# Gate and up products of three SwiGLU layers read their tokens in pieces of 64 or 32 bytes, in another order in each layer

## The chip, the cores and the metric

The kernel runs on one core of one Trainium2 chip. The metric is the time of one execution on the device, in microseconds (us), as the median of several runs. All the data are float32. TensorE multiplies in the fp32r form: a value is split into a high part and a low part, and a product is made of three matmuls, low by high, high by high and high by low.

## The reference, cut to what matters

The program is two blocks over 512 tokens of width 1024. The first block is a convolution mixer and a SwiGLU; the second has two layers, each with an attention and a SwiGLU whose input product passes a causal convolution of width 3 over the tokens:

```python
h = h + swiglu(rmsnorm(h, g_ffn[l]), w_gate[l], w_up[l], w_down[l])   # first block; 1024 -> 2 x 2816 -> 1024
...
u = x @ w_in                                                          # second block, each layer; 1024 -> 5632
up = jnp.pad(u, ((0, 0), (CONV_WIDTH_2 - 1, 0), (0, 0)))
u = sum(conv_w[j] * up[:, j:j + s] for j in range(CONV_WIDTH_2)) + conv_b
g, val = u[..., :D_FF_2], u[..., D_FF_2:]
return (jax.nn.silu(g) * val) @ w_out
```

The products `x @ w_gate`, `x @ w_up` and the two `x @ w_in` are the ones that the change touches. There are three such stages, named gu0, gu1 and gu2 in the kernel.

## The kernel before, in words

Activations lie with channels on the 128 partitions and the 512 tokens along them: `XH` and `XL` hold the high and the low part of the normed tokens as 8 tiles of 128 channels by 512 tokens. Weights come as items. For a gate or up stage an item is 1024 by 128 weights, that is 8 tiles of 128 by 128, and gives one tile of 128 hidden channels by 512 tokens. A stage has 44 items, 22 gates and 22 ups in turn.

Each item passes through a line of engines. SP's queue loads it into `raw` (two buffers), ScalarE copies it to `WH` in fp32r (line 1585), GpSimd writes the rest, `raw` minus `WH`, into `WL` (line 722), and TensorE runs 8 steps of three matmuls each (lines 963 to 965), accumulating in one PSUM bank of 512 columns. `WH` and `WL` have four slots. The semaphore `w_lo` tells TensorE that a half of an item has its low part, `item_done` gives the slot and the bank on, and `bank_read` tells it that the bank was emptied.

What sets the order is the program of each engine, written out by hand. TensorE's is: `stage_in_halves` does the first two items of a stage in halves of 256 tokens, tile by tile as the norm hands them over (lines 1036, 1048 and 1049), and waits there for all 8 tiles of both halves; `whole` then does the other 42 items of the stage over all 512 tokens, of which the first two go to the banks `attended` and the others to `bank`. A whole item is 24 matmuls of 512 columns, so that the three stages have 3 x 42 x 24 = 3024 of them.

The full banks are read by ScalarE (line 1810 in gu0, line 1939 in gu1 and gu2) and by VectorE (line 2408 in gu0, line 2494 in gu1 and gu2); each reader waits for `item_done` or what follows from it, and reads tokens 0 to 511 in order. The hidden tiles are then split into `HH` (ScalarE) and `HL` (GpSimd, line 849), and the down stage reads these.

`whole` is also called for the other products over all tokens (the mixer's input, the output products); `step` is also called by the attention's projections and by the down stages, through `item`.

Of the kernel before, what the change touches and what calls it, by code (L numbers as in the profile page):

```python
# [9 lines left out]
DT = D // P  # L10
# [39 lines left out]
STAGES = {}  # L50
# [14 lines left out]
FIRST_FOX_STEPS = (0, 0, 1, 1, 2, 2, 2, 2, 2, 2, 2, 0)  # L65
DIFF_STEPS = (1, 1, 1, 1, 2, 2, 2, 3, 2, 4, 5, 0)
FIRST_DIFF_STEPS = (1, 2, 1, 1, 1, 1, 1, 1, 1, 2, 4, 0)
PAIRS = (TAPS + 1) // 2
DIAG_CHUNK = 16
EDGE = (TAPS - 1) // 2  # L70
# [107 lines left out]
def two_blocks(nc, A, out):  # L178
    ctx = ExitStack()
    with ctx:  # L180
        def sb(name, shape, dt=F32, stack=None):
            return (stack or ctx).enter_context(nc.sbuf_tensor(name, shape, dt))
# [20 lines left out]
        WH = sb("WH", [P, SLOTS, DT, P], F32R)  # L203
        WL = sb("WL", [P, SLOTS, DT, P], F32R)
# [17 lines left out]
        first = ExitStack()  # L222
# [9 lines left out]
        mixp = sb("mixp", [P, 2, S], stack=first)  # L232
        tap_f = sb("tap_f", [P, 2, 2 * PAIRS], stack=first)
        tap_h = sb("tap_h", [P, 2, 2 * PAIRS], F32R, stack=first)
        tap_l = sb("tap_l", [P, 2, 2 * PAIRS], stack=first)
        two_ones = sb("two_ones", [P, HEAD], stack=first)
        dg_h = sb("dg_h", [P, 2, 2 * PAIRS, HEAD], F32R, stack=first)
        dg_l = sb("dg_l", [P, 2, 2 * PAIRS, HEAD], F32R, stack=first)
        u_f = sb("u_f", [P, 2, EDGE + HALF], stack=first)
# [66 lines left out]
        banks = bank + ob + sc  # L306
# [402 lines left out]
        def _(pool):  # L709
# [81 lines left out]
            for n in range(12):  # L791
# [3 lines left out]
                if 2 <= n < 6:  # L795
                    g, a = divmod((n - 2) * DIAG_CHUNK, 2 * PAIRS)
                    pool.tensor_tensor(dg_l[:, g, a:a + DIAG_CHUNK, :], two_ones[:, :].unsqueeze(1).broadcast_to([P, DIAG_CHUNK, HEAD]),
# [163 lines left out]
        def _(pe):  # L961
            def product(out_, wh, wl, xh, xl, start, stop):
                pe.matmul(out_, wh, xl, start=start, stop=False)  # L963
                pe.matmul(out_, wh, xh, start=False, stop=False)  # L964
                return pe.matmul(out_, wl, xh, start=False, stop=stop)  # L965

            def step(g, b, hi, lo, k0, k, kt, start, stop, turned=False):

                if k == 0:
                    pe.wait_ge(w_lo, g.times(2).n(2 if turned else 1))  # L970
                if k == kt - kt // 2 and not turned:
                    pe.wait_ge(w_lo, g.times(2).n(2))
                s = g.slot(SLOTS)
                mm = product(banks[b][:, :], WH[:, s, k, :], WL[:, s, k, :], hi[:, k0 + k, :], lo[:, k0 + k, :],
                             start and k == 0, stop and k == kt - 1)
                if k == kt - 1:
                    mm.then_inc(item_done, 1)

            def item(g, b, hi, lo, k0, kt, start, stop):

                for k in range(kt):
                    step(g, b, hi, lo, k0, k, kt, start, stop)

            def bank_free(u):
                pe.wait_ge(bank_read[u.slot(2)], u.round(2))

            def whole(name, j, it=0, per=4, x=(XH, XL), apart=False, fed=False):
                u = Nth(STAGES[name][1] + j, it, per)
                if fed:
                    bank_free(u + -2)  # L990
                elif not apart:
                    bank_free(u)
                item(Nth(STAGES[name][0] + j, it, per), u.slot(2) + 2 * apart, *x, 0, DT, True, True)

            def stage(name, hi=XH, lo=XL):

# [80 lines left out]
            def down(name, layer):  # L1077
# [5 lines left out]
                def tile(t, it=0):  # L1083
                    u = Nth(STAGES[name][1] + t, it, 2)
                    bank_free(u)
                    for j in range(4):
                        if t == 0 and j == 3:
                            for q in h_lo:
                                pe.wait_ge(q, (layer + 1) * FT // 2 + OPEN)
                        item(Nth(STAGES[name][0] + 4 * t + j, it, 8), u.slot(2), HH, HL, *down_part(j), j == 0, j == 3)  # L1090
# [112 lines left out]
            for q in range(QT):  # L1203
                pe.wait_ge(x_in[q], 16)
                for b in range(2):
                    if q == QT - 1:
                        pe.wait_ge(bank_read[b], 1)
                    for t in range(4):
                        mm = pe.transpose(x_banks[q][b][:, t * P:(t + 1) * P], xin[:, q, (4 * b + t) * P:(4 * b + t + 1) * P], ident[:, :])
# [134 lines left out]
            def unit_steps(name, u):  # L1344

                turn0 = STAGES[name][1]
                item0 = STAGES[name][0]
                for tile in range(3):
                    for k in range(DT):
                        part, kk = (tile, k) if tile < 2 else (2 + k // 4, k % 4)  # L1350
                        if k == 0 and tile == 0 and u.base == 1 and isinstance(u.it, int):
                            pe.wait_ge(bank_read[0], turn0 // 2 + 1)
                        elif k == 0 and tile == 1 and u.base == 1 and isinstance(u.it, int) and name == "qkv2":
                            pe.wait_ge(bank_read[1], turn0 // 2 + 1)
                        elif k == 0:
                            bank_free(u.times(4, turn0 + tile))
                        step(u.times(4, item0 + part), tile % 2, XH, XL, k - kk, kk, UNIT[part],
                             part < 3, part != 2, tile < 2 and name == "qkv2")
                        yield

            def unit_steps_fed(name, m):

                stage_in_halves(name, m)
                if name == "qkv1":
                    head_gates()
                turn0, item0 = STAGES[name][1], STAGES[name][0]
                for k in range(DT):
                    step(Nth(item0 + 2 + k // 4), 3 if name == "qkv1" else 2, XH, XL, k - k % 4, k % 4, 4, k < 4, k >= 4)

            def turn_v(name, u):  # L1370

                pe.wait_ge(bank_read[0], u.times(4, STAGES[name][1] + 2).round(2, 1))
                turned = bank[1]
                if name == "qkv2" and first_unit(u):
                    turned = ob[1]
                else:
                    bank_free(u.times(4, STAGES[name][1] + 3))
                for q in range(QT):
                    mm = pe.transpose(turned[:, q * P:(q + 1) * P], vt[:, q * P:(q + 1) * P], ident[:, :])
                mm.then_inc(v_turned, 1)  # L1380
# [43 lines left out]
            def weave(steps, slot_work, counts, lead=0, then=lambda: None):  # L1424

                for _ in range(lead):
                    next(steps, None)
                then()
                for sl, count in enumerate(counts):
                    slot_work(sl)  # L1430
                    for _ in range(count):
                        next(steps, None)
                for _ in steps:
                    pass
# [75 lines left out]
            def diff_slot(u):  # L1510
                slot = u.slot(2)
                first = 4 * UNITS

                def work_of(sl):
                    if sl == 3 and first_unit(u):
                        pe.wait_ge(lam_d, 1)
                    if sl == 1 and not first_unit(u):
                        turn_v("qkv2", u)
                    if sl == 2 and not (isinstance(u.it, int) and u.base == 0):
                        mean_square(u + -1)  # L1520
                    if sl < 8:
                        if sl == 0:
                            pe.wait_ge(q_padded, u.times(128).n(128))
                        if sl < 2:
                            pe.wait_ge(k_low[sl], u.n(1))
                        score(sl, u.times(4, first + sl // 2), slot, sl // 2)
                    if sl in (4, 6, 8, 10):
                        i = sl // 2 - 2
                        turn_map(i % 2, u.times(2, first + i // 2), pmap[:, 2 * (i % 2), :], i)
                    if sl == 11:  # L1530
                        for b in range(2):
                            pe.wait_ge(pt_l[b], u.times(2, first + 2).n() + OPEN)
                        pe.wait_ge(bank_read[1], u.times(4, STAGES["qkv2"][1] + 3).round(2, 1))
                        attend(0, slot, u + UNITS)
                    if sl == 12:
                        mean_square(u)
                return work_of
# [6 lines left out]
            def diff_part(iu, au):  # L1544
# [10 lines left out]
                elif first_unit(au):  # L1555
                    def lambda_and_v():
                        pe.wait_ge(lam_a, 1)
                        pe.matmul(tb[0][:, 0:1], ones[0:1, :], lam_row[2], start=True, stop=True).then_inc(lam_b, 1)
                        turn_v("qkv2", au)
                    weave(unit_steps("qkv2", iu), diff_slot(au), FIRST_DIFF_STEPS, DT, lambda_and_v)  # L1560
                else:
# [1102 lines left out]
```

## Time and profile before

| | us |
|---|---|
| median of 3 runs | 1810.76 |
| lowest and highest of them | 1810.24, 1812.06 |
| profiled execution, its own time | 1809.7 |
| its span | 1807.9 |
| TensorE busy | 1762.5 (97%) |
| weight loads busy (beside the matmuls) | 1476.5 (82%) |
| GpSimd, ScalarE, VectorE busy | 1032.6, 796.2, 765.0 |

The granted clock of TensorE was 0.995 of full speed over the whole execution. A busy time of matmuls is that of records which overlap: a record lasts from the issue until the last column has left the array, and the next matmul starts well before. The pace of a run of matmuls is therefore read from the distance of their starts, not from their length.

### The profile page before, as it was taken

What the parts mean: (1) busy time and instruction counts of PE and PEld (TensorE: products, weight loads), DVE (VectorE), ACT (ScalarE), POOL (GpSimd) and SP (SyncE); (2) the same over time, 40 slices, a digit from 0 to 9 for tenths busy, and PEclk for the clock granted to TensorE, in tenths of its full rate; (3) what the DMA queues carried; (4) which work ended last, traced back from release to release, by engine and by line L of the source; (5) the groups of instructions that cost most, each with busy time, mean ns of one, the idle gap of its engine ahead of it and who ended that gap; (6) DMA issues with size and microseconds to landing.
All of it is one profiled execution on the core that took longest, in us unless ns stands there. A gap on an engine that the chain in (4) does not pass through costs nothing.

```text
span 1807.9 us, 26859 instructions
## 1 busy us (share of the span) xinstructions
PE 1762.5 (97%) x8755; PEld 1476.5 (82%) x8755; DVE 765.0 (42%) x1382; ACT 796.2 (44%) x1674; POOL 1032.6 (57%) x926
## 2 busy tenths in 40 slices
PE   8999999999999999999999999999999999999997
PEld 6879888888887888788888888877777888888887
DVE  7963000002235556553333322487875533333224
ACT  5644323322245555464444422555565644444231
POOL 7966555555562333466666655655554666666651
PEclk9999999999999999999999999999999999999999
DMA  4312333323334454323333233233322233332332
GB/s 154 92 47 83 104 93 93 97 87 108 91 99 106 126 134 117 87 82 98 100 93 93 87 105 94 76 94 82 86 76 76 66 110 98 93 100 83 105 91 98
DMA packets 327252, 171.94 MB, mean 95 GB/s; under 512 B 43458, under 2 KB 316948, under 8 KB 327188
## 3 DMA queue, kind: packets, MB, share of 16 engines
q1 hardware_dynamic: 327172, 171.12, 33.7%
q8 instruction: 35, 0.57, 0.1%
q14 instruction: 29, 0.24, 0.0%
q10 hardware_dynamic: 16, 0.00, 0.0%
HBM read 152.15 MB, written 2.10 MB: 85 GB/s over the span
## 4 chain that ended last, share of the span: by engine, by line
PE 85%; DVE 9%; ACT 2%; issue 1%; POOL 1%; DMA 1%; SPq 0%; DVEq 0%; ACTq 0%
PE bank L963 23%; PE bank L965 23%; PE bank L964 23%; DVE score L2246 3%; PE attended L963 2%; PE attended L965 2%; PE attended L964 2%; PE turned L1404 1%; PE attended L1420 1%; PE bank L1036 1%; PE bank L1048 1%; DVE small L2434 1%; ACT pmap L1841 1%; PE bank L1049 0%; DMA raw<-in_a_w_in 0%
## 5 line engine op out<-in xcount | busy, mean ns | idle before, releaser
L722 POOL TENSOR_TENSOR WL<-raw,WH 128x512 fp32r<-128x512 f32 (+3 forms) x656 | 778.0, 1208 | 542.0 <-ACT WH L1585 539.7
L963 PE MATMUL bank<-XL,WH 128*128 128x512 f32 x1432 | 568.9, 397 | 3.7 <-DVE work L2557 1.2
L965 PE MATMUL bank<-XH,WL 128*128 128x512 f32 x1432 | 557.8, 390 | 0.0
L964 PE MATMUL bank<-XH,WH 128*128 128x512 f32 x1432 | 557.1, 389 | 0.0
L1585 ACT ACTIVATE WH<-raw 128x512 fp32r<-128x512 f32 (+3 forms) x656 | 338.4, 566 | 298.0 <-PE bank L965 177.9
L965 PEld LDWEIGHTS bank<-XH,WL 128*128 128x128 f32 x1432 | 269.4, 188 | 57.0
L963 PEld LDWEIGHTS bank<-XL,WH 128*128 128x128 f32 x1432 | 269.9, 188 | 55.9 <-DVE work L2557 1.5
L964 PEld LDWEIGHTS bank<-XH,WH 128*128 128x128 f32 x1432 | 270.1, 189 | 50.2
L963 PE MATMUL bank<-HL,WH 128*128 128x512 f32 (+1 forms) x528 | 198.6, 376 | 0.0
L965 PE MATMUL bank<-HH,WL 128*128 128x512 f32 (+1 forms) x528 | 198.4, 376 | 0.0
L964 PE MATMUL bank<-HH,WH 128*128 128x512 f32 (+1 forms) x528 | 198.4, 376 | 0.0
L849 POOL TENSOR_TENSOR HL<-hid,HH 128x512 f32 x66 | 85.1, 1289 | 70.7 <-ACT HH L1801 70.7
L2346 DVE SCALAR_TENSOR_TENSOR xres<-xres,bank 128x512 f32 (+1 forms) x27 | 18.6, 687 | 251.0 <-PE bank L965 248.3
L965 PEld LDWEIGHTS bank<-HH,WL 128*128 128x128 f32 x528 | 99.4, 188 | 18.1
L964 PEld LDWEIGHTS bank<-HH,WH 128*128 128x128 f32 x528 | 99.4, 188 | 18.0
L963 PEld LDWEIGHTS bank<-HL,WH 128*128 128x128 f32 x528 | 99.4, 188 | 17.9
L1841 ACT ACTIVATE pmap<-score,small 128x128 f32<-128x128 f32 (+3 forms) x128 | 67.3, 526 | 103.3 <-DVE small L2434 103.0
L2408 DVE TENSOR_TENSOR hid<-bank,act_g 128x512 f32<-128x512 f32 x21 | 14.5, 692 | 207.5 <-PE bank L965 203.9
L1939 ACT ACTIVATE hid<-bank,par 128x512 f32<-128x512 f32 x42 | 32.7, 778 | 143.5 <-PE bank L965 143.5
L2494 DVE SCALAR_TENSOR_TENSOR hid<-bank,par,hid 128x511 f32<-128x511 f32 x42 | 31.5, 750 | 150.7 <-ACT hid L1939 150.5
L2494 DVE SCALAR_TENSOR_TENSOR act_g<-bank,par,act_g 128x511 f32<-128x511 f32 x42 | 31.5, 751 | 133.8 <-ACT act_g L1939 133.8
L2434 DVE TENSOR_REDUCE small<-score 128x1 f32<-128x128 f32 (+3 forms) x128 | 62.2, 486 | 35.5 <-PE score L1389 23.6
(366 smaller groups left out, 2523.1 us busy)
## 6 DMA issues: line engine op xcount, KB each, us to landing
raw<-in_ffn_w_in SPq DMA_DIRECT2D x88, 512.0 KB, 3.7
raw<-in_w_gate SPq DMA_DIRECT2D x22, 512.0 KB, 3.7
raw<-in_w_up SPq DMA_DIRECT2D x22, 512.0 KB, 3.7
raw<-in_ffn_w_out SPq DMA_DIRECT2D x28, 384.0 KB, 3.2
raw<-in_ffn_w_out SPq DMA_DIRECT2D x28, 320.0 KB, 3.1
raw<-in_a_w_in SPq DMA_DIRECT2D x16, 512.0 KB, 3.9
raw<-in_kv_w SPq DMA_DIRECT2D x32, 256.0 KB, 2.9
raw<-in_w_in SPq DMA_DIRECT2D x12, 512.0 KB, 3.8
```

The costliest lines, as they stand in the source:

```text
L722: pool.tensor_tensor(wl, x, wh, ALU.subtract).then_inc(w_lo, 1)
L849: pool.tensor_tensor(HL[:, bass.ds(it * 2 + j, 1), :], hid[:, j:j + 1, :], HH[:, bass.ds(it * 2 + j, 1), :].bitcast(F32), ALU.subtract).th ...
L963: pe.matmul(out_, wh, xl, start=start, stop=False)
L964: pe.matmul(out_, wh, xh, start=False, stop=False)
L965: return pe.matmul(out_, wl, xh, start=False, stop=stop)
L1585: act.activation(wh, x, ACT.Copy).then_inc(w_hi, 1)
L1841: act.activation(pmap[:, n % 4, 0:k], sc[c][:, 0:k], ACT.Exp, bias=small[:, n % 4:n % 4 + 1], accum_out=small[:, 4 + n % 4:5 + n % 4]).the ...
L1939: act.activation(dst[:, j, :], ff_banks(it, j)[side][:, :], ACT.Identity, bias=ff_par(layer - 1, 3, n), scale=ff_par(layer - 1, 2, n)).the ...
L2246: ins = dve.scalar_tensor_tensor(out=vconv[:, c, :] if j == TAPS - 2 else part, in0=upad[:, c, j:j + S], scalar=tap(j, c), in1=part, op0=A ...
L2346: dve.scalar_tensor_tensor(out=r, in0=r, scalar=factor, in1=src[j][:, :].rearrange("p (a s) -> p a s", a=1), op0=ALU.mult, op1=ALU.add).th ...
L2434: dve.tensor_reduce(small[:, n % 4:n % 4 + 1], sc[c][:, 0:(n // 2 + 1) * P], AX_X, ALU.max, negate=True).then_inc(mx[c], 1)
L2494: own.link(dve.scalar_tensor_tensor(out=dst[:, j, 1:], in0=src[:, 0:S - 1], scalar=ff_par(layer - 1, 1, n), in1=dst[:, j, 1:], op0=ALU.mul ...
```

## The change

`step` and `item` get a parameter `order`, and `whole` sets it by the stage's name. For gu0, gu1 and gu2 the moving operand (`XH` or `XL`, 512 tokens) and the output (the bank's 512 columns) are both seen through the same rearrangement, so each token's column still lands at its own place in the bank. Only the order in time changes in which the 512 columns of a matmul are read, multiplied and written:

- gu0: pieces of 16 tokens (64 bytes); the 16 even pieces first, then the 16 odd ones. 32 runs.
- gu1: pieces of 16 tokens; the first of the first half (256 tokens), the first of the second half, the second of the first half, and so on. 32 runs.
- gu2: pieces of 8 tokens (32 bytes); the 32 even pieces first, then the 32 odd ones. 64 runs.

The number of matmuls, their weights, their banks, their semaphores and all other engines' programs are the same. The first two items of each stage (`stage_in_halves`) and all other stages keep the order of the tokens.

```diff
+CHUNKS = {"gu0": "even chunks, odd chunks", "gu1": "first half, second half in turn",
+          "gu2": "even short chunks, odd short chunks"}
...
+            def in_order(x, order):
+
+                if order == "tokens":
+                    return x
+                if order == "even chunks, odd chunks":
+                    return x.rearrange("p (a b c) -> p b a c", b=2, c=16)
+                if order == "even short chunks, odd short chunks":
+                    return x.rearrange("p (a b c) -> p b a c", b=2, c=8)
+                return x.rearrange("p (h a c) -> p a h c", h=2, c=16)
+
+            def step(g, b, hi, lo, k0, k, kt, start, stop, turned=False, order="tokens"):
...
-                mm = product(banks[b][:, :], WH[:, s, k, :], WL[:, s, k, :], hi[:, k0 + k, :], lo[:, k0 + k, :],
+                mm = product(in_order(banks[b][:, :], order), WH[:, s, k, :], WL[:, s, k, :],
+                             in_order(hi[:, k0 + k, :], order), in_order(lo[:, k0 + k, :], order),
                              start and k == 0, stop and k == kt - 1)
...
-            def item(g, b, hi, lo, k0, kt, start, stop):
+            def item(g, b, hi, lo, k0, kt, start, stop, order="tokens"):
...
-                    step(g, b, hi, lo, k0, k, kt, start, stop)
+                    step(g, b, hi, lo, k0, k, kt, start, stop, order=order)
...
-                item(Nth(STAGES[name][0] + j, it, per), u.slot(2) + 2 * apart, *x, 0, DT, True, True)
+                item(Nth(STAGES[name][0] + j, it, per), u.slot(2) + 2 * apart, *x, 0, DT, True, True,
+                     CHUNKS.get(name, "tokens"))
```

## Rows read from the trace of the kernel before

**Rows 1.** The page: busy time of the engines, share of the span, instructions.
```profile
PE 1762.5 (97%) x8755; PEld 1476.5 (82%) x8755; DVE 765.0 (42%) x1382; ACT 796.2 (44%) x1674; POOL 1032.6 (57%) x926
```
**Rows 2.** The page: the chain that ended last, by engine.
```profile
PE 85%; DVE 9%; ACT 2%; issue 1%; POOL 1%; DMA 1%; SPq 0%; DVEq 0%; ACTq 0%
```
**Rows 3.** Busy time by window, 220 us of gu0, gu1 and gu2; then PEclk, DMA share, GB/s.
```profile
170.00:390.00 220.00, 220.00 (x973) 182.21 (x972) 13.90 (x21) 68.13 (x124) 130.61 (x104) 1.00 0.33 97
810.00:1030.00 220.00, 220.00 (x972) 182.16 (x971) 75.37 (x102) 97.49 (x163) 140.50 (x104) 1.00 0.33 97
1450.00:1670.00 220.00, 220.00 (x972) 182.25 (x971) 73.87 (x100) 96.35 (x161) 138.95 (x102) 1.00 0.32 95
```
**Rows 4.** Waits inside gu1 (840 to 1000 us): total, times, longest.
```profile
POOL WL L722 <- ACT WH L1585: 57.6, 29, 2.9
ACT hid L1939 <- PE bank L965: 53.8, 15, 3.6
```
**Rows 5.** Timeline of TensorE: first whole item's matmul of gu0, first of the down stage.
```profile
168.49 0.40 PE L963 MATMUL attended<-XL,WH 128*128 128x512 f32 x1
...
397.00 0.39 PE L963 MATMUL bank<-HL,WH 128*128 128x512 f32 x1
```
**Rows 6.** The same timeline, two matmuls of gu0 with 50 between them.
```profile
329.68 0.39 PE L963 MATMUL bank<-XL,WH 128*128 128x512 f32 x1
...
341.24 0.39 PE L963 MATMUL bank<-XL,WH 128*128 128x512 f32 x1
```
**Rows 7.** The same timeline in down0, matmuls of 256 columns, 34 between first and last.
```profile
501.72 0.28 PE L963 MATMUL bank<-HL,WH 128*128 128x256 f32 x1
501.83 0.28 PE L964 MATMUL bank<-HH,WH 128*128 128x256 f32 x1
...
505.91 0.28 PE L965 MATMUL attended<-HH,WL 128*128 128x256 f32 x1
```
**Rows 8.** The same timeline in the mixer's convolution, 41 between first and last.
```profile
84.10 0.28 PE L963 MATMUL attended<-u_l,dg_h 128*128 128x256 f32 x1
...
89.11 0.28 PE L963 MATMUL attended<-u_l,dg_h 128*128 128x256 f32 x1
```
**Rows 9.** Groups on ScalarE: 1200 to 1380 us, then 840 to 1000 us.
```profile
L1585 ACT ACTIVATE WH<-raw 128x512 fp32r<-128x512 f32 x32 | 18.3, 624 | 0.0
L1585 ACT ACTIVATE WH<-raw 128x512 fp32r<-128x512 f32 x58 | 33.1, 620 | 0.0
```

More of the change, by code:

```diff
@@ L965, in product @@
                 return pe.matmul(out_, wl, xh, start=False, stop=stop)
-            def step(g, b, hi, lo, k0, k, kt, start, stop, turned=False):
+            def in_order(x, order):
[7 more added lines that the diff above has]
+            def step(g, b, hi, lo, k0, k, kt, start, stop, turned=False, order="tokens"):
                 if k == 0:
```

## The prediction

> **What bounds the kernel now.** I read the page's busy times first: TensorE is busy for 97% of the span, the next engine (GpSimd) for 57% [rows 1]. Then the chain that ended last: 85% of it is TensorE's own work, 9% VectorE's [rows 2]; VectorE's part lies in the mixer and between stages, not where the change is. So I went to the stages that the change touches, by windows: in each of three stretches of 220 us TensorE is busy for all of the 220 us at a granted clock of 1.00, the higher of its two levels, 2.4 GHz, while GpSimd, the busiest of those that feed it or read from it, works for 131 to 141 us of them, ScalarE for at most 97 and VectorE for at most 75; the DMA share is a third [rows 3]. The waits in gu1 say the same: GpSimd and ScalarE stand waiting (57.6 and 53.8 us in 160), and TensorE has no wait there [rows 4]. In these stages time is the number of matmuls times their pace, and nothing else.
>
> **The pace, step by step.** The record of a matmul (0.39 us) overlaps the next, so I take distances of starts. From the first whole item of gu0 to the first matmul of the down stage there are 42 x 24 = 1008 matmuls in 397.00 - 168.49 = 228.5 us, 226.7 ns each [rows 5]. In the middle of the stage 51 take 11.56 us, again 226.7 ns [rows 6]: the pace is even, with no hole at the ends of items. The three windows hold 972 or 973 matmuls in 220 us each, the same pace in all three layers [rows 3]. The 3024 matmuls that get another order take 3024 x 0.2267 = 685.5 us, 38% of the span. Matmuls of 256 columns start 4.19 / 35 = 119.7 ns apart [rows 7]. The 256 further columns so cost 107 ns, 0.418 ns each, which is one clock at 2.4 GHz (0.417), and 226.7 - 213.3, about 13 ns, are left per matmul, whatever its length.
>
> **What the change removes and adds.** It removes no instruction and adds none: the same 3024 matmuls, weight loads and semaphores, the same columns, the same bytes. The order is fixed when the program is built, so no register has to be computed. What changes is the pattern of addresses: 31 jumps within each matmul of gu0 and gu1 (32 runs of 16 columns) and 63 in gu2 (64 runs of 8), in the read of the tokens and at once in the write of the bank.
>
> **What a jump costs.** No matmul of the trace reads or writes within one instruction in more than one run, so I bound it from both sides. Below: nothing, since a column already costs no more than one clock, and no row has a faster one; the only thing that could shrink is the 13 ns per matmul (a rival below). Above, the nearest row, though far: the start of a whole matmul, with its new addresses, weights and output, costs those 13 ns. Were a jump as dear as that, a matmul of gu0 would grow by 31 x 13 = 403 ns. Two rows are nearer. In the mixer's convolution the moving operand starts one float later with every pair of taps, so most of its matmuls start off any boundary of 8, 16 or 64 bytes; 42 of them take 5.01 us, 119.3 ns each, no more than the 119.7 of the matmuls that start on one [rows 7, 8]. Where the read starts makes no difference. And on ScalarE, the weight copies between 1200 and 1380 us, most of which read their 512 elements in runs of 32 (128 bytes) with jumps between them, take 624 ns against 620 for copies that read whole rows of 128 [rows 9]: 4 ns for some 15 jumps, on another engine at another rate. Both lie nearest to nothing, and I take 0 ns per jump: 3024 x 0 = 0.
>
> One rule of the Trainium skill speaks against this. The page "PSUM — Partial Sum Buffer" (Specifications) says that the cachelines are of 8 bytes and that any pattern that isn't contiguous slows matmuls significantly, with no figure. "Advanced Engine Details and Errata" (PSUM Cachelines) has the same sentence, but adds that every two consecutive elements should be contiguous for best throughput; pieces of 8 or 16 floats hold to that. By the first reading the slow rival below is what happens; by the second the sum stays 0. No row of this trace writes PSUM in pieces, so the trace takes neither side.
>
> **What is not touched.** Nobody needs the tokens in an order: TensorE has waited for all 8 tiles of both halves before the first whole item, and each reader of a bank waits for the end of all 24 matmuls and reads token by token at the old addresses. The stores of the hidden tiles, GpSimd's and ScalarE's splits and SP's loads keep their times, and their cover is wide: GpSimd has about 80 of 220 us free [rows 3]. If TensorE slowed down, they would only get more; if it ran 6% faster (the whole 13 ns), GpSimd's 141 of 220 us would still fit into 207. In the three matmuls of a step, and from one step to the next, the same column comes round again after 512 others, as before, so that adding onto a column waits no longer. Nothing is late next because nothing leaves.
>
> **The sum.** Span 1807.9 + 0; the profiled execution's own time is 1.8 above its span (1809.7), and the median of the runs shown is 1.1 above that: 1807.9 + 0 + 1.8 + 1.1 = 1810.8 us. A measurement of this kernel tells from no change what is over about 0.2%, 3.6 us (1807.2 to 1814.4).
>
> **Rivals.**
> 1. Slower, at every jump. If the address generator or one of the memories loses one clock per jump, that is 0.417 x 31 = 12.9 ns per matmul in gu0 and gu1 and 26.3 ns in gu2: 2016 x 12.9 = 26.0 us and 1008 x 26.3 = 26.5 us, 52.5 us together, and the time is 1863.3; at two clocks per jump it is 1915.8. Nothing covers it, as TensorE never waits in these stages [rows 4]. It decides early: 3.6 us over 3024 matmuls is 1.2 ns per matmul, less than a tenth of a clock per jump. For it: the matmul already takes in a column per clock and has no slack to hide a jump in. Against it: the shifted starts of the convolution and ScalarE's runs [rows 8, 9].
> 2. Slower in one layer only. If only short runs cost, because 8 columns are too few to fetch ahead, gu2 alone pays 26.5 us: 1837.3. If only the far jumps of gu1 (256 columns to and fro) cost a clock, it is 13.0 us: 1823.8. For it: gu2's runs are a quarter of the nearest row's 32 elements. Against: the same as above.
> 3. Faster. If the 13 ns per matmul come from a clash of the end of one matmul's reads or writes with the start of the next at the other end of the bank or tile, another order could take part of them away: at most 3024 x 13.3 = 40.3 us, 1770.5. Against it: they are the same for 256 columns as for 512, for tokens that start shifted, and where the bank changes between `bank` and `attended` [rows 5, 7, 8]; and all three orders still begin at column 0 and end at column 511.
> 4. The change does not do what it says: the builder makes two matmuls of 256 columns out of each. The pieces of 120 ns then give 2 x 119.7 - 226.7 = 12.7 ns more per matmul, 38 us: 1849. The number of TensorE's instructions would show it at once.
>
> **How the numbers follow.** Nothing moves: 0.66. Every jump costs: 0.12. One layer alone costs: 0.13 (0.08 for short runs, 0.05 for a smaller price in any one). The builder splits: 0.01. Faster by the 13 ns: 0.08. This gives faster 0.08, within 0.2% 0.66, slower 0.26. The forecast is the likeliest case, 1810.8. The range begins at the bound of what can be told, 1807, and goes to 1838, where short runs alone cost a clock: 0.66 + 0.13 = 0.79, with a little of rival 3. The likeliest case's own range is 1809 to 1813.
>
> **What would show each step.** The distance of the starts of L963 to L965 in the three stages: 226.7 ns and 228.5 us for the 42 items if I am right, in all three; 239.6 ns in gu0 and gu1 and 253.0 in gu2 under rival 1; only gu2 off under rival 2; less than 226.7 under rival 3. TensorE's instructions stay at 8755 and the granted clock at 1.00, GpSimd's and ScalarE's waits keep their sizes, and the stages outside the three keep their lengths to 0.5 us. I would be wrong if the pace in any of the three stages moved by more than 1.2 ns per matmul, or if the clock, which was 1.00 with the same numbers in the order of the tokens, fell in one of them.

## The result, and the profile after

The changed kernel takes 1843.03 us in the median of 4 runs (1841.34 to 1843.67), the kernel before 1811.41 us (1810.24 to 1813.4) in the runs beside it: a ratio of 1.0172, 95% interval 1.0154 to 1.0190. The forecast was 1810.8 us, no change, with a range up to 1838. It was wrong; the kernel is 31.6 us slower.

The page after shows the same instructions and the same shape of work. TensorE has 8755 matmuls as before, with 35 us more busy time, and its share of the chain goes from 85% to 86% [rows 1, 2]:

```profile
span 1841.9 us, 26859 instructions
PE 1797.1 (98%) x8755; PEld 1483.5 (81%) x8755; DVE 765.9 (42%) x1382; ACT 795.6 (43%) x1674; POOL 1029.8 (56%) x926
...
PE 86%; DVE 9%; ACT 2%; issue 1%; DMA 1%; POOL 1%; SPq 0%; DVEq 0%; ACTq 0%
```

Busy time by window, 220 us in gu0, gu1 and gu2 of the changed kernel. TensorE is again busy throughout at a clock of 1.00, but where the windows before held 973, 972 and 972 matmuls [rows 3], these hold 919, 918 and 948:

```profile
170.00:390.00 220.00, 220.00 (x919) 172.71 (x918) 13.62 (x20) 64.53 (x118) 122.12 (x98) 1.00 0.32 93
825.00:1045.00 220.00, 220.00 (x918) 174.44 (x917) 70.49 (x96) 92.00 (x154) 132.67 (x97) 1.00 0.32 93
1475.00:1695.00 220.00, 220.00 (x948) 178.01 (x947) 73.19 (x99) 95.55 (x160) 135.50 (x100) 1.00 0.33 96
```

TensorE's timeline after, the first whole item's matmul of each stage and the first of the down stage behind it, as in [rows 5]:

```profile
168.90 0.40 PE L965 MATMUL attended<-XL,WH 128*128 128x512 f32 x1
...
410.82 0.39 PE L965 MATMUL bank<-HL,WH 128*128 128x512 f32 x1
...
819.51 0.40 PE L965 MATMUL attended<-XL,WH 128*128 128x512 f32 x1
...
1061.43 0.39 PE L965 MATMUL bank<-HL,WH 128*128 128x512 f32 x1
...
1468.91 0.40 PE L965 MATMUL attended<-XL,WH 128*128 128x512 f32 x1
...
1703.15 0.39 PE L965 MATMUL bank<-HL,WH 128*128 128x512 f32 x1
```

The 1008 matmuls of a stage take 241.9, 241.9 and 234.2 us, that is 240.0, 240.0 and 232.4 ns each against 226.7 before. The extra is 13.3, 13.3 and 5.7 ns: 13.4 + 13.4 + 5.7 = 32.5 us. That is the whole result, within the interval (1.54% to 1.90% of 1811 us is 28 to 34 us). The two profiled spans differ by 34.0 us: what comes ahead of gu0 is 0.4 us longer after, the stretch between gu0 and gu1 2.4 us longer, and the one between gu1 and gu2 1.4 us shorter. The change doesn't touch them, and from run to run the two stretches take between 406 and 409 us anyway (406.0 and 409.1 in e2). The 13.3 ns are 32 clocks of 2.4 GHz, as many as gu0 and gu1 have runs; but gu2, with twice as many runs, pays 14 clocks. One clock per jump can't be the rule.

### The profile page after: what moved, and what is told of

Read it like the earlier page. It is cut to its first block, busy times and chain, and to the rows that moved or that the text cites. A ratio compares the mean times of both kernels' runs of the same rounds, so it can differ in the third digit from the quotient of the medians.

```text
span 1841.9 us, 26859 instructions
## 1 busy us (share of the span) xinstructions
PE 1797.1 (98%) x8755; PEld 1483.5 (81%) x8755; DVE 765.9 (42%) x1382; ACT 795.6 (43%) x1674; POOL 1029.8 (56%) x926
## 4 chain that ended last, share of the span: by engine, by line
PE 86%; DVE 9%; ACT 2%; issue 1%; DMA 1%; POOL 1%; SPq 0%; DVEq 0%; ACTq 0%
PE bank L965 23%; PE bank L967 23%; PE bank L966 23%; DVE score L2260 3%; PE attended L965 2%; PE attended L966 2%; PE attended L967 2%; PE turned L1418 1%; PE attended L1434 1%; PE bank L1050 1%; PE bank L1062 1%; PE bank L1063 1%; PE score L1401 0%; PE score L1402 0%; DVE small L2603 0%
## 5 line engine op out<-in xcount | busy, mean ns | idle before, releaser
L965 PE MATMUL bank<-XL,WH 128*128 128x512 f32 x1432 | 578.9, 404 | 3.7 <-DVE work L2571 1.2
L967 PE MATMUL bank<-XH,WL 128*128 128x512 f32 x1432 | 568.4, 397 | 0.0
L966 PE MATMUL bank<-XH,WH 128*128 128x512 f32 x1432 | 567.5, 396 | 0.0
```

## The experiments

Each experiment is a single run, except two that are named. In the fences of windows the columns are the window, its length, TensorE's busy time with the count of matmuls, the granted clock, the DMA share and GB/s. A count takes in one or two matmuls that only reach over an edge of the window, so nanoseconds per matmul are taken from the distance of starts in the timeline: in the token order, 226.7. `("even, odd", n)` is the order of gu0 with pieces of n columns, `("halves in turn", n)` that of gu1; a pair gives the read's order and the write's.

**The read alone, and the write alone.**

```diff
-    mm = product(in_order(banks[b][:, :], order), ..., in_order(hi[:, k0 + k, :], order), in_order(lo[:, k0 + k, :], order),
+    mm = product(in_order(banks[b][:, :], order[1]), ..., in_order(hi[:, k0 + k, :], order[0]), in_order(lo[:, k0 + k, :], order[0]),
+# e1: order[1] = tokens in the three stages; e2: order[0] = tokens
```

> Only the read of the tokens takes the new orders (even and odd pieces of 16 in gu0, halves in turn in gu1, even and odd pieces of 8 in gu2); the bank is written in token order, so tokens land permuted. In the changed kernel a matmul of the three stages started every 240.0, 240.0 and 232.5 ns, against 226.7 before. If the price is the read's, this kernel has the same three paces and a time near 1843 us. If it is the bank write's, all three stages stay at 226.7 ns and the time is near 1811. If it comes from both being off the token order, or adds from both sides, the paces lie between.

> Only the write of the bank takes the new orders; the tokens are read in token order, so tokens land permuted. Price of the write: 240.0, 240.0 and 232.5 ns and near 1843 us. Price of the read: 226.7 ns in all three and near 1811 us. The two kernels' extra nanoseconds should add up to 13.3, 13.3 and 5.8 if the sides add.

Measured: 1840.95 us with the read alone, 1808.85 with the write alone, 1809.72 for the kernel before. The windows of e1, then of e2:

```profile
200.00:380.00 180.00, 180.00 (x752) 1.00 0.31 90
850.00:1030.00 180.00, 180.00 (x751) 1.00 0.31 90
1500.00:1680.00 180.00, 180.00 (x777) 1.00 0.33 96
```

```profile
200.00:380.00 180.00, 180.00 (x796) 1.00 0.33 96
850.00:1030.00 180.00, 180.00 (x796) 1.00 0.32 94
1500.00:1680.00 180.00, 180.00 (x796) 1.00 0.32 94
```

The read pays everything (752, 751, 777 against 752, 752 and 776 in the changed kernel over the same windows) and the write nothing (796; before, 796, 795 and 796). This pair settles which side it is.

**The order or the layer.**

```diff
+CHUNKS = {"gu0": ("even, odd", 8), "gu1": ("even, odd", 16), "gu2": ("halves in turn", 16)}   # read and write alike
```

> The three orders change places, read and write alike: even and odd pieces of 8 in gu0, even and odd pieces of 16 in gu1, halves in turn by 16 in gu2. If the order makes the price, gu0 goes to 232.5 ns and gu1 and gu2 to 240.0, and the time stays within 1 us of 1843. If it is the layer (what the other engines do beside it: VectorE works 13.6 of 220 us in gu0 and 73 in gu2), gu0 stays at 240.0 and gu2 at 232.5.

Measured: 1842.91 us. The price moved with the order, 776 matmuls, 232.4 ns each, now in gu0:

```profile
200.00:380.00 180.00, 180.00 (x776) 1.00 0.33 96
850.00:1030.00 180.00, 180.00 (x751) 1.00 0.31 91
1500.00:1680.00 180.00, 180.00 (x751) 1.00 0.31 91
```

So it isn't what the other engines do beside it: VectorE's load differs fivefold between the layers and the paces don't.

**Longer and shorter runs.**

```diff
+# e4: "even, odd" by 32, 64, 128 in gu0, gu1, gu2
+# e5: read only: "even, odd" by 4 and by 2, "halves in turn" by 4; down stages, write only: "even, odd" by 4 and by 2, "halves in turn" by 2
+# e6: "halves in turn" by 8, 32, 64; down stages: "even, odd" by 8 and by 16, every fourth piece of 16
```

> Even pieces and then odd pieces again, but longer: 32 columns in gu0 (16 runs), 64 in gu1 (8 runs), 128 in gu2 (4 runs), read and write alike. If a jump costs one clock and short runs escape for a reason of their own, the extra is 16, 8 and 4 clocks: 233.3, 230.0 and 228.3 ns. If an order out of token order costs a fixed 32 clocks per matmul, all three are at 240.0. If only pieces of exactly 16 meet something, all three are at 226.7.

> Read only, shorter runs: even and odd pieces of 4 in gu0, of 2 in gu1, halves in turn by 4 in gu2 (banks written in token order). Write only, in the down stages: pieces of 4, of 2, and halves in turn by 2 (hidden tiles read in token order). Tokens land permuted. So far the read's price was 0 for runs of 64 and 128 columns, 24 clocks of 2.4 GHz for 32, 32 for 16, 14 for 8. If the price goes by run length and falls again below 16, all three are at or under 232.5 ns. If short runs are dearer once less than a line is used, gu1 (8 bytes) is far above 240. The write was free down to 8 columns; if it stays so, the down stages keep 226.7 ns.

> Read and write alike: halves in turn by 8 in gu0, by 32 in gu1, by 64 in gu2; in the down stages, on the hidden tiles, even and odd pieces of 8, of 16, and every fourth piece of 16. If run length alone makes the price: 232.5, 236.7, 226.7, and 232.5, 240.0, 240.0 ns. If it depends on how soon the read comes back to the same place modulo 256 bytes (theory of interleaved memories), halves in turn by 8 comes back after 8 columns where even and odd by 8 comes back after 32, and gu0 is dearer than 232.5; every fourth piece of 16 comes back after 16 and is at or above 240.

Measured: 1822.01, 2063.89 and 1853.9 us. In ns per matmul, the token order being 226.7:

| run length | even, odd | halves in turn |
|---|---|---|
| 128 | 226.7 | |
| 64 | 226.7 | 226.7 |
| 32 | 236.7 | 236.7 |
| 16 | 240.0 | 240.0 |
| 8 | 232.4 | 243.3 |
| 4 | 233.3 | 250.0 |
| 2 | 451.1 | |

The hidden tiles of the down stages give 233.3 for even and odd by 8, 240.0 by 16 and 239.5 for every fourth piece of 16. Windows of e4 (gu0 at 32 columns, gu1 at 64), and of e5 (gu1 at 2 columns, then the down stages with write pieces of 2):

```profile
200.00:380.00 180.00, 180.00 (x762) 1.00 0.32 93
850.00:1030.00 180.00, 180.00 (x796) 1.00 0.33 96
```

```profile
850.00:1030.00 180.00, 180.00 (x401) 1.00 0.16 47
...
1275.00:1335.00 60.00, 60.00 (x266) 1.00 0.35 102
1940.00:2000.00 60.00, 60.00 (x267) 1.00 0.36 103
```

None of the three cases that were named ahead for e4 came true: 32 columns cost 10 ns, 64 and 128 nothing. Three things follow. In these orders runs of 64 columns, 256 bytes, are free and shorter ones are not. Run length alone doesn't make the price: at 8 columns the two orders differ by 11 ns, at 4 by 17. And the bank can be written in pieces of 8 bytes at the full pace (266 or 267 in 60 us, with starts 226.7 ns apart), while reading in pieces of 8 bytes doubles the time.

**A constant step between runs.** Here the read is a single pattern, so many columns at a constant step through all the token tiles; the bank is written in order. The data are not the reference's.

```diff
+            def strided(x, k, order, turn):
+                c, step_ = order[turn]
+                return x.rearrange("p k s -> p (k s)")[:, 0:S // c * step_].rearrange("p (a c) -> p a c", c=step_)[:, :, 0:c]
```

> Read only: 512 columns as 32 runs of 16 at one constant step through all of the token tiles (data and so results are not the reference's). The four items of each round of the loop have a step and a source line of their own: 16 (no jump), 32, 48, 64 columns in gu0; 80, 96, 112, 128 in gu1; runs of 8 with steps 16, 24, 32, 40 in gu2. Theory A, run length alone: all jumping ones of gu0 and gu1 at 240 ns, all of gu2 at 232.5. Theory B, memories interleaved over 64 columns (256 bytes), price by how soon the read comes back to the same place: steps 64 and 128 come back at once and are the dearest (above 243), steps 48, 80 and 112 visit all four sixteens in turn and cost nothing, 226.7; 32 and 96 come back every second run, 240. In gu2 steps 24 and 40 near 226.7, 16 near 232.5, 32 dearer.

> The same with runs of 32 and steps 64, 96, 128, 160 in gu0; runs of 64 and steps 128, 192, 256, 320 in gu1; runs of 4 and steps 8, 12, 16, 20 in gu2. Theory A: gu0 all at 236.7, gu1 all at 226.7, gu2 all at 233.4. Theory B: in gu0 steps 96 and 160 at 226.7, 64 and 128 at 236.7; gu1 all at 226.7, since each run takes in the whole 64 columns; in gu2 steps 12 and 20 near 226.7, 16 far dearer than 8.

Measured: 1850.71 and 1830.36 us; what counts are the items. TensorE's timeline in gu0 of e9, the first matmul of successive items of 24 (L973 is step 16, L977 step 32, L981 step 48, L985 step 64):

```profile
203.01 0.40 PE L973 MATMUL bank<-XL,WH 128*128 128x512 f32 x1
...
208.47 0.40 PE L977 MATMUL bank<-XL,WH 128*128 128x512 f32 x1
...
214.24 0.40 PE L981 MATMUL bank<-XL,WH 128*128 128x512 f32 x1
...
219.94 0.41 PE L985 MATMUL bank<-XL,WH 128*128 128x512 f32 x1
...
225.75 0.40 PE L973 MATMUL bank<-XL,WH 128*128 128x512 f32 x1
```

The items take 5.46, 5.77, 5.70 and 5.81 us: 227.5, 240.4, 237.5 and 242.1 ns per matmul. The same lines in gu1, with steps 80, 96, 112 and 128:

```profile
901.86 0.40 PE L977 MATMUL bank<-XL,WH 128*128 128x512 f32 x1
...
907.62 0.40 PE L981 MATMUL bank<-XL,WH 128*128 128x512 f32 x1
...
913.32 0.41 PE L985 MATMUL bank<-XL,WH 128*128 128x512 f32 x1
...
919.14 0.40 PE L973 MATMUL bank<-XL,WH 128*128 128x512 f32 x1
...
924.60 0.40 PE L977 MATMUL bank<-XL,WH 128*128 128x512 f32 x1
```

96, 112 and 128 give 240.0, 237.5 and 242.5, and 80 (the last item) 227.5: each as the step that is 64 smaller, within what starts printed to 10 ns can tell. A step of 80 makes 31 jumps over 64 columns each and costs what no jump costs. At these steps the price has a period of 64 columns, 256 bytes. Runs of 32 say the same: steps 64, 96, 128, 160 give 236.7, 228.3, 236.7, 228.3 ns; runs of 64 take 226.7 at steps 128, 192, 256 and 320. (The item without a jump takes 227.6 here, among dearer ones, where a whole stage of such items takes 226.7; single items are to be held against 227.6.) Theory A (run length alone) is refuted. Theory B had the period right and the sizes partly wrong: it wanted steps 48 and 112 free, and they cost 10 ns; and short runs give 233.4, 239.8, 233.4, 266.4 (8 columns, steps 16, 24, 32, 40) and 233.5, 227.2, 228.2, 266.4 (4 columns, steps 8, 12, 16, 20), where it had 24, 40 and 20 free, 32 dearer than 16, and with 4 columns a step of 16 far dearer than 8.

**The weight load beside it.** First by its width, and with matmuls of 256 columns:

```diff
-                mm = product(banks[b][:, :], WH[:, s, k, :], WL[:, s, k, :], ...
+                mm = product(banks[b][0:m, :], WH[:, s, k, 0:m], WL[:, s, k, 0:m], ...       # e7, e11: m = 64
+                for h in range(2):                                                           # e8, e11: two passes over the item
+                    c = slice(h * HALF, (h + 1) * HALF)
```

> The weight loads of the gate and up items in the two banks named bank have 64 columns, not 128 (64 of the 128 hidden channels are left out). gu0 in token order, gu1 with even and odd pieces of 16, gu2 with pieces of 8. If the price is a clash of the token read with the weight load beside it, half as long a load halves it: gu1 near 233, gu2 near 229.6, and gu0 falls under 226.7 if the 13 ns of token order are such a clash too. If the price is the token read's alone: 226.7, 240.0, 232.5.

> Each gate and up item in two passes of 256 columns, so twice the matmuls and weight loads; even and odd pieces of 8 in gu0, 16 in gu1, 32 in gu2, within each half. In token order 256 columns took 119.7 ns. If the price is one per run or per column, it halves: 122.6, 126.4 and 124.7 ns. If it is a clash with the weight load, which is as long as before, it stays nearly whole: 125.5, 133 and 129.7 ns.

> Gate and up items in two passes of 256 columns with weight loads of 64 columns in the banks named bank (64 of 128 hidden channels are left out): token order in gu0, even and odd pieces of 16 in gu1, of 32 in gu2. With loads of 128 columns the three orders took 119.7 to 120.0, 120.0 and 117.4 ns, so the price of the 512-column matmuls was not there. If a weight load of 128 columns bounded them and hid the price, the narrow loads show it: gu1 and gu2 6 ns or more above gu0. If the price is really absent at 256 columns, all three stay within 2 ns of each other.

Measured: 1833.56, 1840.47 and 1834.1 us. With 512 columns and narrow loads the paces are 230.0 (token order, dearer than with wide loads), 240.0 (pieces of 16, as before) and 231.1 (pieces of 8). So half as long a load doesn't halve the price. The windows of e8 (128 weight columns; even and odd by 8, 16, 32), then of e11 (64; token order, even and odd by 16, by 32), all of matmuls of 256 columns:

```profile
200.00:380.00 180.00, 180.00 (x1531) 1.00 0.32 92
850.00:1030.00 180.00, 180.00 (x1503) 1.00 0.31 90
1500.00:1680.00 180.00, 180.00 (x1537) 1.00 0.32 93
```

```profile
200.00:380.00 180.00, 180.00 (x1591) 1.00 0.33 95
850.00:1030.00 180.00, 180.00 (x1503) 1.00 0.31 90
1500.00:1680.00 180.00, 180.00 (x1502) 1.00 0.31 90
```

With narrow loads token order takes 113.3 ns for 256 columns and the two other orders 120.0, a price of 6.7 ns. With loads of 128 columns pieces of 8, 16 and 32 take 117.8, 120.0 and 117.3, and token order, read from the down stage, 120 [rows 7]: no order is dearer than token order there, and two are cheaper. So whether the price shows goes by the load beside it. Why is not shown; the length of a wide load isn't simply the bound, or 117.3 could not have been reached. What it means for the prediction is plain: a row of 256 columns beside a load of 128, as [rows 7] and [rows 8] are, shows nothing of a price that is there at 512 columns.

Then by its place:

```diff
+                return x[:, s].rearrange("p k n -> p (k n)")[:, k * P + at:(k + 1) * P + at]   # weights from column at
```

> Read only (data and results are not the reference's). gu0: token order, one run of 512 from column 4, 1, 16 and 33. gu1: runs of 16 at step 32 from column 0, 4, 8 and 16. gu2: runs of 32 at steps 40, 48, 80, 112. Theory C: the price belongs to a run that does not begin, modulo 64 columns, where the last one ended. Then gu0 is at 226.7 to 228 for all four, gu1 at 240 for all four, and in gu2 steps 48 and 112, which are the same modulo 64, are alike and dear, with 80 dear too. If instead the start of a matmul has to lie on a line of 4 or 16 columns, the offsets 1 and 33 are dearer than 16, and gu1's offsets differ.

> The token read started at column 4, 1, 16, 33 cost 231.7, 236.4, 229.8, 236.0 ns where column 0 costs 226.7 to 227.8. Here the weight read is shifted (data and results are not the reference's). gu0: tokens in order from column 0, weights from column 4, 1, 16, 32 of their tile. gu1: even and odd pieces of 16, weights from column 0, 4, 16, 32. gu2: tokens and weights shifted by the same 4, 1, 16, 33. Theory C (the token read alone): gu0 all at 226.7 to 227.8, gu1 all at 240, gu2 at 231.7, 236.4, 229.8, 236.0. Theory D (the token read and the weight load of the next matmul meet in the same interleaved memory, and token order from an aligned start is the one in which they keep out of each other's way): gu0 rises to the prices of the opposite shifts, gu1 changes with the shift, and gu2 falls back towards 226.7 where both are shifted alike.

Measured: 1838.17 and 1840.88 us. Token order, 512 columns in one run, ns per matmul by where the reads start:

| tokens from column | weights from column | ns |
|---|---|---|
| 0 | 0 | 226.7 (a stage), 227.6 (an item of e9) |
| 4, 1, 16, 33 | 0 | 231.6, 236.4, 229.6, 236.0 |
| 0 | 4, 1, 16, 32 | 233.2, 232.4, 233.1, 232.4 |
| 4, 1, 16, 33 | the same | 231.5, 237.6, 227.9, 237.7 |

The timeline in gu2 of e15, both shifted alike (L977 by 1, L981 by 16):

```profile
1526.42 0.40 PE L977 MATMUL bank<-XL,WH 128*128 128x512 f32 x1
...
1532.13 0.39 PE L981 MATMUL bank<-XL,WH 128*128 128x512 f32 x1
...
1537.60 0.40 PE L985 MATMUL bank<-XL,WH 128*128 128x512 f32 x1
```

24 matmuls take 5.71 us shifted by 1 (237.9 ns) and 5.47 us shifted by 16 (227.9). Theory C is refuted: by e14 already, as it had all four shifted token reads between 226.7 and 228, and by e15, where with the token read untouched a shift of the weight read alone costs 5 to 6 ns, and shifting both by 16 columns, 64 bytes, takes the price of either shift away. So the two reads of TensorE affect each other, and for this shift it goes by where one stands against the other. But theory D isn't shown whole: with shifts by 4 alike the time doesn't fall back, and with both reads started at 1 or at 33, off a multiple of 4 columns (16 bytes), it stays dear. In the dear orders the clash explains less: with pieces of 16 the loads' width changed nothing (240.0 with 64 and with 128), and the place of the weights little (240.0, 243.6, 242.0, 240.0 for 0, 4, 16, 32). Token offsets 0, 4, 8 and 16 of runs of 16 at step 32 gave 240.0, 231.5, 240.3 and 239.5, so the start at 4 is far cheaper than the others, and nothing here says why. Runs of 32 at steps 40, 48, 80, 112 gave 233.3, 239.2, 239.9, 238.4, where 48 and 112, equal modulo 64, are nearly alike.

**Another order at no price, and an attempt to gain.** These two were timed over 12 and 11 runs.

```diff
+# e13: "even, odd" by 64 in gu0, "halves in turn" by 64 in gu1, "even, odd" by 128 in gu2, read and write alike
+# e12, on the kernel before: all matmuls of 256 columns in stage_in_halves and half_item
+                return x.rearrange("p (a b c) -> p b a c", b=2, c=32)
```

> All three stages out of token order, read and write alike, but in pieces that are whole multiples of 64 columns (256 bytes): even and odd 64 in gu0, halves in turn by 64 in gu1, even and odd 128 in gu2. If leaving the 256-byte sequence is the whole price, all three run at 226.7 ns and the ratio to the kernel before is within 0.1% of 1. If being out of token order costs anything beside it, the ratio shows it: one clock per jump would be 7 x 0.42 ns x 3024, 6 us or more.

> The kernel before, with every matmul of 256 columns of the halves (some 1150 of them: the first two items and the last two tiles of the stages) reading and writing even and odd pieces of 32. That order took 117.4 ns where token order took 119.7 to 120.0. If the gain carries over, 1150 x 2.3 to 2.6 ns is 2.6 to 3.0 us less, a ratio near 0.9985. If those stretches wait for their inputs, or the gain was of the long even rows of such matmuls only, the time is that of before; a price as with 512 columns would add up to 10 ns each, 11 us.

Measured: e13 1810.84 us, ratio to the kernel before 1.0002 (0.9993 to 1.0011), with all three paces back at 226.7. Reading out of token order is free in these three orders, whose pieces are whole multiples of 256 bytes. e12 1810.4 us, ratio 1.0000 (0.9991 to 1.0009): the order that took 117.3 ns in the item loop of e8 takes 120.0 in the halves of the down stage, as token order does, and no time is gained. Why the two places differ is open, and no run has token order at 256 columns with wide loads in the item loop; no version here beats the kernel before.

## Why the prediction was wrong

**The bound.** Right: the time of these stages is the count of matmuls times their pace. TensorE was busy for all of the windows after as before, nothing covered the price, and the extra of the three stages is the extra of the kernel. That the stages outside would keep their lengths to 0.5 us was too narrow: two stretches between them moved by 2.4 and 1.4 us, as they do in runs that don't touch them.

**What a jump costs** is the step that failed: "I take 0 ns per jump: 3024 x 0 = 0". Measured, the token read costs 13.3 ns more per matmul in gu0 and gu1 and 5.7 in gu2, and 32.5 us came in place of 0. The two rows that it leaned on could not show the price. The convolution's matmuls with shifted starts have 256 columns and weight loads of 128 [rows 8]. At that size pieces of 16 take 120.0 ns (e8), no more than token order, though at 512 columns they cost 13.3 and at 256 with loads of 64 they cost 6.7 (e11). "Where the read starts makes no difference" is wrong at 512 columns: a shifted start costs 2 to 9 ns there (e14). And the mean of 119.3 hid something that the convolution's own rows show. Its starts lie from 0.11 to 0.13 us apart, one by one, where in [rows 7] all distances but the first are 0.12:

```profile
84.59 0.28 PE L964 MATMUL attended<-u_h,dg_h 128*128 128x256 f32 x1
84.70 0.29 PE L965 MATMUL attended<-u_h,dg_l 128*128 128x256 f32 x1
84.83 0.28 PE L963 MATMUL attended<-u_l,dg_h 128*128 128x256 f32 x1
```

ScalarE's runs of 128 bytes [rows 9] are another engine's read: they cost it 4 ns in 620, and the same length costs TensorE 10.0 in 227 (e4). So the likely case rested on one row of another size and one of another engine.

**The 13 ns "per matmul, whatever its length"** were worked out from one row of each length, both beside loads of 128 [rows 6, 7]. They are no fixed part of a matmul. Over one clock per column, token order takes 6.7 ns at 256 columns with loads of 64 (e11) and 16.7 at 512 with the same loads (e7); at 256 with loads of 128, pieces of 32 take 10.7 (e8). So "the same for 256 columns as for 512" was no argument against rival 3, which the measured time excludes. In clocks, 226.7 ns are 17 for 16 columns and the 240.0 of gu0 and gu1 are 18 for 16; why is not shown.

**The write** was rightly put at nothing (e2 at 64 and 32 bytes, e5 down to 8). The page "PSUM — Partial Sum Buffer" of the Trainium skill (Specifications), by which any pattern that isn't contiguous slows matmuls significantly, isn't borne out here: pieces of 64, 32, 16 and 8 bytes were written at 226.7 ns (e2, e5), which agrees with "Advanced Engine Details and Errata" (PSUM Cachelines), two consecutive elements. That page of the Trainium skill (SBUF Cachelines) also asks for at least two hits on a line of 16 bytes to take in the access latency. For this read that is not enough: runs of 2 floats had two, and took 451.1 ns against 226.7 (e5).

**The rivals.** Rival 1 (one clock per jump) comes within a clock of gu0 and gu1, 31 against 32 (its 239.6 ns against 240.0), but that is luck, since its mechanism is refuted: gu2 should have paid 63 clocks and paid 14, and steps of 80 cost nothing for 31 jumps. Its time, 1863, is 20 us too high. Rival 2 named the wrong layer: short runs alone were to cost, and gu2 was the cheapest; its other case, gu1's far jumps alone, is out too, as gu0 paid the same. Rival 3 (faster) and rival 4 (two matmuls out of one) are excluded, the latter by 8755 matmuls. The paces of the three stages, named ahead as the test, told at once that no case of the forecast was true as it stood.

**The chances.** 0.26 on slower was too little. A column already took all of its clock, with no slack, and a changed address pattern had no row at 512 columns in its favour; with no row, the two sides deserved more even chances and the range the 1863 of rival 1.

**What is settled and what is open.** Shown: the price is the token read's and not the write's; it goes with the order and not with the layer; it repeats every 256 bytes of step in the steps compared; whole pieces of 256 bytes are free; and the token read and the weight read affect each other (shifts by 16: 229.6, 233.1, and 227.9 together). Not shown: what makes the price in the changed kernel's own orders. No rule here gives the sizes, such as 8 columns cheaper than 16 in even and odd, the 266 ns at steps 40 and 20, or the 231.5 at offset 4, and whether the clash with the weight read has a part in them is open. An interleaved memory fits the period, but no run shows the memory itself.

## What to carry to other kernels

Before a cost of nothing is read off a row, ask whether that row is of the same size and has the same work beside it: here, matmuls of 256 columns beside loads of 128 showed nothing of a read that costs 13.3 ns at 512. Look at single distances and not at their mean alone. For matmuls like these (fp32r, 512 columns, 128 weight columns) read the moving operand in whole runs of 256 bytes that start on a multiple of 256 bytes in their tile, and start the weights at the start of theirs; the bank may be written in pieces of 8 bytes at no price. Where a change of pattern has no row at the same size, give slower nearly even chances and let one stage carry one variant each, so that a single trace tells them apart.

## What the runs showed of the hardware that was not expected

- fp32r moving reads, 512 columns, 128 weight columns: 226.7 ns in order; 236.7, 240.0, 232.4, 233.3 and 451.1 ns in runs of 32, 16, 8, 4 and 2 columns (even and odd; e1 to e5).
- The price of runs of 16 repeats every 64 columns of step (e9): 240.4 and 240.0 at 32 and 96, 242.1 and 242.5 at 64 and 128, 227.5 at 16 and 80.
- Writing the bank in pieces of 8 bytes: 226.7 ns, no price (e5).
- 256 columns in order: 120 ns with weight loads of 128 columns [rows 7], 113.3 with 64 (e11). Yet 512 columns in order take 230.0 ns with loads of 64 (e7), more than the 226.7 with 128.
- Token order read from column 1, 4, 16 or 33 of its tile takes 236.4, 231.6, 229.6 and 236.0 ns per matmul of 512 columns, against 227.6 for an item without shift (e14, e9).
